# Filling the expert gate tables in DRAM with indirect adding transfers from GpSimd, in place of one-hot matmuls on TensorE

## The chip, the cores and the metric

The kernel runs on one core of a Trainium2 chip, as one program. The metric is the device time of one execution in microseconds (us). Names of engines: PE is TensorE, DVE VectorE, ACT ScalarE, POOL GpSimd; SP is the engine that issues most DMAs.

## The reference

Two layers, each an attention mixer and then a feed-forward of experts, on one sequence of 256 tokens and 2048 features. The change lies in the second part (`peer_ffn`), which for each token picks 16 of 16,384 experts for each of 8 heads:

```python
s1, i1 = lax.top_k(s[..., 0, :], PEER_TOPK)        # 16 best of 128 keys, side 1
s2, i2 = lax.top_k(s[..., 1, :], PEER_TOPK)        # side 2
cand = (s1[..., :, None] + s2[..., None, :]).reshape(b, L, PEER_HEADS, PEER_TOPK * PEER_TOPK)
cidx = (i1[..., :, None] * N_KEYS + i2[..., None, :]).reshape(...)
top_s, pos = lax.top_k(cand, PEER_TOPK)            # 16 of the 256 pairs
eidx = jnp.take_along_axis(cidx, pos, axis=-1)
g = jax.nn.softmax(top_s, -1)
...
h = jnp.einsum('td,tkd->tk', xt, u[et])
a = gt * jax.nn.gelu(h, approximate=False)
return jnp.einsum('tk,tkd->td', a, v[et])
```

The kernel does not gather rows of `u` and `v`. It computes the hidden value of every expert for every token, multiplies it by a table of gates (zero for each pair of token and expert that was not chosen, the sum of the gates where several heads chose the same one), and multiplies the product with the whole of `v`.

## The kernel before, in words

All large products are made in float32 from two rounded parts: ACT rounds a tile to its high part (`split_hi`, `hi<-raw`), DVE subtracts to get the low part (`split_lo`, `lo<-raw,hi`), and PE multiplies high and low parts. Weights come in tiles of 1 MB (`raw`, four buffers); each tile is two halves. SP loads a tile as soon as the halves that lay in its buffer have been split (`load` waits on `lo_done`), and splits run four halves ahead of PE.

Of a layer, two stages matter here. In the **u stage**, 128 tiles of `u_t` are taken, 256 halves: for each half PE runs 8 matmuls of 512 columns (L464) and 8 of 256 (L466). A body is 8 halves, so the stage has 32 bodies; `quarter` is 8 bodies. Every tile gives the hidden values of 128 experts, which go through Gelu on ACT and to `gelu_scratch` in DRAM (L954). In the **v stage**, 128 tiles of `v_t` are taken; for each half PE runs 12 matmuls of 512 columns (L691 to L693). For each tile SP first fetches the stored Gelu values and a piece of the gate table (`side`, L395 and L396), and DVE multiplies them (`product`), ACT and DVE split the product (`a_high`, `a_low`). SP issues in program order, so the loads of `v_t` stand behind the first four pairs of side loads.

The gates are made inside the u stage, in blocks `b` of 128 tokens. In quarter 1 DVE routes block 0, one head per body (`route_body`: top 16 of each side, top 16 of 256 sums, lookup of the key numbers), a loop over heads, for which POOL copies each head's scores (`copy_keys`). In quarter 2 the table of block 0 is built: the key numbers and gates are transposed on PE (L674) to `sel_t`; then for each pair of tokens, one of 64 `gate_step`s: POOL writes the one-hot rows of the first key (`first_keys`, L1094 and L1097), DVE those of the second key times the gate (`second_keys`, L1567), ACT their low part (`low_part`, L970), PE multiplies them (L656, two matmuls of 256 columns), ACT and DVE put the 128 by 128 result into `gates` in SBUF (`place_gates` L963, `add_low` L1575). Quarters 3 and 4 do the same for block 1, and in quarter 3 ACT also turns the finished block 0 over and stores it to DRAM in 16 pieces (`stage`, L977). The order on each engine is that of the program text; semaphores tie the engines together. At the end of the u stage DVE has the last three `add_low`s and then the first products ahead of PE's first matmul of the v stage.

Of the kernel before, what the change touches and what calls it, by code (L numbers as in the profile page):

```python
# [8 lines left out]
F32 = mybir.dt.float32  # L9
# [118 lines left out]
def build(nc, x_in, w_in, w_out, wq, keys, u_t, v_t, ln, sinks, lamp, subg, layer_consts,  # L128
# [10 lines left out]
    a_dram = nc.dram_tensor("gates_scratch", [NKEY, P, P], F32, kind="Internal").ap()  # L139
    g_dram = nc.dram_tensor("gelu_scratch", [NKEY, P, L], F32, kind="Internal").ap()  # L140

    with ExitStack() as ctx:
# [10 lines left out]
        SCR_OFFSET = 16512 + 4 * (NB * D + 2 * DC * L + NRAW * TILE + 2 * NSPLIT * HT + 16384)  # L153
# [6 lines left out]
        key_cols = [small[:, 64 + i * 2:66 + i * 2] for i in range(4)]  # L160
# [6 lines left out]
        key_now = sb("key_now", [P, 2, NKEY])  # L167
# [33 lines left out]
        assert at <= 16384  # L201
# [6 lines left out]
        gates = arena[:, :].rearrange("p (t i) -> p t i", i=NKEY)  # L208

# [23 lines left out]
        TG = 2  # L233
        STEPS = P // TG
        quarter = N_U // BODY // 4
        assert quarter == PH
        STEPS_OF = {0: (0,), 1: (1,), 2: (2, 3), 3: (4,), 4: (5, 6), 5: (7,), 6: (8,)}
        PER_BODY = sum(len(k) for k in STEPS_OF.values())
        BUILD = quarter - 1
        assert 1 + BUILD * PER_BODY == STEPS  # L240
        RING = 3

        def steps_at(b, i, j):
            if i == 0:
                return [b * STEPS] if j == BODY - 1 else []
            return [b * STEPS + 1 + (i - 1) * PER_BODY + k for k in STEPS_OF.get(j, ())]

        def built_at(b, i, j):
            return [n + RING for n in steps_at(b, i, j) if n + RING < (b + 1) * STEPS]

        PIECES = 16
        ROWS = NKEY // PIECES
        one_hots = nc.alloc_sbuf_tensor_at("one_hots", [P, 2048], F32R, offset=SCR_OFFSET)
        more_hots = sb("more_hots", [P, 512], F32R)
        oh1 = [t[:, i * 256:(i + 1) * 256].rearrange("p (t n) -> p t n", n=NKEY) for t in (one_hots, more_hots) for i in range(2)]
        oh2 = [one_hots[:, 512 + i * 512:512 + (i + 1) * 512].rearrange("p (t r n) -> p t r n", r=2, n=NKEY) for i in range(RING)]
        gate_rows = [scr[:, i * 1024:(i + 1) * 1024].rearrange("p (i t) -> p i t", t=P) for i in range(2)]
        gate_hi, gate_share = cand[:, 0:P], cand[:, P:2 * P]
# [39 lines left out]
        with nc.Block() as block:  # L298
            for layer in range(DEPTH):
# [37 lines left out]
                def _(sp):  # L337
# [48 lines left out]
                    with sp.Fori(0, 4 * quarter) as i:  # L386
                        for j in range(NRAW):
                            load(tiles(u_t), AT_U, i, j)
# [1422 lines left out]
```

## Time and profile before

| | |
|---|---|
| time, median of 3 runs | 3876.05 us (3875.96 to 3878.84) |
| span of the profiled execution | 3879.7 us |
| its own timed value | not among the three; only its span is known |
| PE busy | 3830.7 us, 99% |
| DVE, ACT, POOL busy | 71%, 56%, 15% |
| moved by DMA | 807.13 MB, mean 208 GB/s |

The profile is one execution recorded by the hardware. Times are from the start of the span. Busy PE time is that of the pipelined matmuls, whose recorded durations overlap: their real pace is the distance between starts. The granted clock of PE is given as a share of 2.4 GHz.

### The profile page before, as it was taken

The numbers are of one execution on the slowest core, as the hardware profiler recorded it, in microseconds if no ns is written. First come the engines' busy times: TensorE is split into PE (matmuls) and PEld (weight loads), VectorE is DVE, ScalarE is ACT, GpSimd is POOL, SyncE is SP. The second block draws the span as 40 slices with busy tenths as digits, with TensorE's granted clock in tenths as the row PEclk, the third lists the DMA queues.
The fourth block names the chain that finished last, engine by engine and source line by source line (L and its number), as shares of the span: only waits on it lengthen the run. The fifth ranks groups of instructions, "written<-read, shape, count | busy, mean of one in ns | idle before, by whom it ended". The sixth has DMA issues, their size and how long they took to land.

```text
span 3879.7 us, 62117 instructions
## 1 busy us (share of the span) xinstructions
PE 3830.7 (99%) x19796; PEld 3244.8 (84%) x19796; DVE 2745.4 (71%) x5272; ACT 2172.5 (56%) x3609; POOL 575.7 (15%) x844
## 2 busy tenths in 40 slices
PE   9999999999999999999999999999999999999997
PEld 7778888888888888888787788888888888888886
DVE  7765688778877666666687666887788766666666
ACT  5674455776676444444456644457767764444443
POOL 1000000750174000000011000017402730000000
PEclk9999999999999999999999999999999999999999
DMA  6445566557755666666654455665577556666664
GB/s 227 161 144 195 185 204 211 196 197 248 252 193 203 231 231 228 227 227 230 226 171 155 141 207 176 212 212 194 200 251 247 190 208 230 231 230 228 227 228 168
DMA packets 244209, 807.13 MB, mean 208 GB/s; under 512 B 24928, under 2 KB 157536, under 8 KB 159328
## 3 DMA queue, kind: packets, MB, share of 16 engines
q1 hardware_dynamic: 173920, 754.87, 55.6%
q10 hardware_dynamic: 70144, 50.35, 4.0%
q8 instruction: 88, 1.44, 0.1%
q14 instruction: 57, 0.47, 0.0%
HBM read 752.69 MB, written 52.43 MB: 208 GB/s over the span
## 4 chain that ended last, share of the span: by engine, by line
PE 94%; DVE 4%; ACT 1%; DMA 0%; issue 0%; POOL 0%; ACTq 0%; DVEq 0%; SPq 0%
PE bank L464 26%; PE bank L466 13%; PE bank L691 12%; PE bank L692 12%; PE bank L693 12%; PE bank L478 5%; PE bank L480 5%; PE bank L479 5%; PE bank L656 2%; DVE lo L1143 1%; PE bank L506 1%; PE bank L519 1%; PE bank L535 0%; PE bank L633 0%; PE bank L491 0%
## 5 line engine op out<-in xcount | busy, mean ns | idle before, releaser
L1143 DVE TENSOR_TENSOR lo<-raw,hi 128x1024 fp32r<-128x1024 f32 x1312 | 1616.8, 1233 | 937.2 <-ACT hi L746 913.4
L746 ACT ACTIVATE hi<-raw 128x1024 fp32r<-128x1024 f32 x1312 | 1387.2, 1060 | 1335.4 <-PE bank L693 758.6
L464 PE MATMUL bank<-xhl,hi 128*128 128x512 f32 x4608 | 1188.7, 393 | 0.5
L464 PEld LDWEIGHTS bank<-xhl,hi 128*128 128x128 f32 x4608 | 814.0, 189 | 135.0 <-DVE gelu_out L1444 1.3
L691 PE MATMUL bank<-hi,xhl 128*128 128x512 f32 x2048 | 798.3, 390 | 4.5 <-DVE xhl L1599 4.5
L692 PE MATMUL bank<-lo,xhl 128*128 128x512 f32 x2048 | 798.1, 390 | 0.0
L693 PE MATMUL bank<-hi,xhl 128*128 128x512 f32 x2048 | 798.0, 390 | 0.0
L466 PEld LDWEIGHTS bank<-xhl,lo 128*128 128x128 f32 x4608 | 654.9, 190 | 62.8
L466 PE MATMUL bank<-xhl,lo 128*128 128x256 f32 x4608 | 671.6, 282 | 0.0
L691 PEld LDWEIGHTS bank<-hi,xhl 128*128 128x128 f32 x2048 | 385.2, 188 | 85.6 <-issue 4.4
L693 PEld LDWEIGHTS bank<-hi,xhl 128*128 128x128 f32 x2048 | 385.2, 188 | 80.2
L692 PEld LDWEIGHTS bank<-lo,xhl 128*128 128x128 f32 x2048 | 385.1, 188 | 80.0
L478 PE MATMUL bank<-hi,xhl 128*128 128x512 f32 (+1 forms) x896 | 360.1, 402 | 2.3 <-DVE xhl L1161 2.3
L480 PE MATMUL bank<-hi,xhl 128*128 128x512 f32 (+1 forms) x896 | 349.9, 391 | 0.0
L479 PE MATMUL bank<-lo,xhl 128*128 128x512 f32 (+1 forms) x896 | 348.6, 389 | 0.0
L1097 POOL TENSOR_SCALAR more_hots<-iota_k,small 128x128 fp32r<-128x128 f32 x256 | 229.5, 909 | 12.1
L1097 POOL TENSOR_SCALAR one_hots<-iota_k,small 128x128 fp32r<-128x128 f32 x256 | 225.9, 895 | 12.2
L947 ACT ACTIVATE gelu_out<-bank 128x256 f32<-128x256 f32 x256 | 98.7, 385 | 193.4 <-PE bank L466 159.5
L478 PEld LDWEIGHTS bank<-hi,xhl 128*128 128x128 f32 x896 | 169.0, 189 | 37.8 <-issue 4.7
L480 PEld LDWEIGHTS bank<-hi,xhl 128*128 128x128 f32 x896 | 168.8, 188 | 35.7
L479 PEld LDWEIGHTS bank<-lo,xhl 128*128 128x128 f32 x896 | 169.4, 189 | 31.0
L970 ACT ACTIVATE one_hots<-one_hots,cand 128x128 fp32r<-128x128 f32 x512 | 171.0, 394 | 36.6 <-ACT gelu_out L952 36.6
(165 smaller groups left out, 2571.5 us busy)
## 6 DMA issues: line engine op xcount, KB each, us to landing
raw<-u_t SPq DMA_DIRECT2D x256, 1024.0 KB, 5.0
raw<-v_t SPq DMA_DIRECT2D x256, 1024.0 KB, 4.8
raw<-w_in SPq DMA_DIRECT2D x80, 1024.0 KB, 4.9
raw<-w_out SPq DMA_DIRECT2D x32, 1024.0 KB, 4.8
raw<-wq SPq DMA_DIRECT2D x32, 1024.0 KB, 4.8
gelu_scratch<-gelu_out ACTq DMA_DIRECT2D x256, 128.0 KB, 3.8
scr<-gelu_scratch SPq DMA_DIRECT2D x256, 128.0 KB, 4.5
gates_scratch<-scr ACTq DMA_DIRECT2D x32, 512.0 KB, 4.6
```

The costliest lines, as they stand in the source:

```text
L464: pe.matmul(acc[:], w, xhl[:, c, :, :].rearrange("p a t -> p (a t)"), start=(c == 0), stop=False)
L466: last = pe.matmul(acc[:, L:2 * L], w, xh[:, c, :], start=False, stop=(c == DC - 1))
L478: pe.matmul(banks[b][:, 0:width], st_h, mh, start=(c == first_c), stop=False)
L479: pe.matmul(banks[b][:, 0:width], st_h, ml, start=False, stop=False)
L480: last = pe.matmul(banks[b][:, 0:width], st_l, mh, start=False, stop=(c == last_c))
L691: pe.matmul(y, a_h, vh, start=start, stop=False)
L692: pe.matmul(y, a_h, vl, start=False, stop=False)
L693: last = pe.matmul(y, a_l, vh, start=False, stop=stop)
L746: act.activation(hi[j % NSPLIT][:], half, ACT.Copy).then_inc(hi_done, 1)
L970: last = act.activation(oh2[s % RING][:, t, 1, :], oh2[s % RING][:, t, 0, :].bitcast(F32), ACT.Identity, scale=gate_share[:, col:col + 1])
L1097: last = pool.tensor_scalar(oh1[p][:, t, :], iota_k[:], key_cols[p][:, t:t + 1], None, ALU.is_equal)
L1143: dve.tensor_tensor(lo[j % NSPLIT][:], half, hi[j % NSPLIT][:].bitcast(F32), ALU.subtract).then_inc(lo_done, 1)
```

## The change: tables filled by GpSimd's adding transfers

There is now one gate table of 128 x 128 x 256 float32 per layer, in DRAM, for both token blocks. SP fills it with zeros in quarter 1 (16 transfers of 1 MB from an SBUF region of zeros, two per body). DVE routes block 0 in quarter 1 and block 1 in quarter 2, its 16 bodies written out head by head and reading the scores where they lie. After each block DVE turns the chosen key numbers into addresses (`slots`: expert number times 256 plus token), and POOL issues for each of the 128 selections (8 heads x 16) an indirect transfer of 128 single weights, one per token, which adds them in DRAM. Since two heads may choose the same expert, the 16 transfers of a head wait for those of the head before. Transposes, one-hot rows, `gate_step`s, placing, adding and staging are gone on all engines. In the v stage `gate_in` is 128 x 256 from DRAM, and `product` is one instruction instead of two.

```diff
-    a_dram = nc.dram_tensor("gates_scratch", [NKEY, P, P], F32, kind="Internal").ap()
+    gate_dram = [nc.dram_tensor(f"gates_scratch{i}", [NKEY, P, L], F32, kind="Internal").ap() for i in range(DEPTH)]
...
+        zeros = arena[:, 15360:16384]
...
+        ZERO_TILES = 8
+        N_ZERO = NKEY // ZERO_TILES
+        N_SCATTER = 16 * PK
...
+                    def zero(n):
+
+                        tables = gate_dram[layer][bass.ds(n * ZERO_TILES, ZERO_TILES)]
+                        rows = tables.rearrange("i p t -> (i p t)").rearrange("(a r c) -> a r c", a=P, c=1024)
+                        sp.dma_start(rows, zeros.unsqueeze(1).to_broadcast([P, ZERO_TILES * L // 1024, 1024])).then_inc(zeroed, 16)
...
+                    with sp.Fori(0, quarter) as i:
                         for j in range(NRAW):
                             load(tiles(u_t), AT_U, i, j)
-                    sp.wait_ge(gates_out, 16 * PIECES)
+                            if j % 2:
+                                zero(i * 2 + j // 2)
+                    with sp.Fori(quarter, 4 * quarter) as i:
+                        for j in range(NRAW):
+                            load(tiles(u_t), AT_U, i, j)
+                    for s in scattered:
+                        sp.wait_ge(s, PH * N_SCATTER)
...
+                        sp.dma_start(gate_in[j], gate_dram[layer][bass.ds(m, 1)].rearrange("a p t -> (a p) t")
+                                     ).then_inc(side_got[j], 16)
...
-                    def gate_step(s):
...
-                            build_gates(b, 0, j)
...
+                        pool.memset(zeros, 0.0).then_inc(zeros_set, 1)
...
-                    def first_keys(s, p, first=False):
...
+                    def scatter(b, h):
+
+                        if h:
+                            pool.wait_ge(scattered[b], h * N_SCATTER)
+                        for k in range(h * PK, (h + 1) * PK):
+                            pool.indirect_dma_start(out=gate_dram[layer].rearrange("i p t -> (i p t)").unsqueeze(1),
+                                                    out_offset=bass.IndirectOffsetOnAxis(ap=slots[:, b, k:k + 1], axis=0),
+                                                    in_=sel[:, 2, b, k:k + 1], in_offset=None,
+                                                    bounds_check=NE * L - 1, compute_op=ALU.add).then_inc(scattered[b], 16)
+
+                    pool.wait_ge(zeroed, 16 * N_ZERO)
...
+                        pool.wait_ge(routed, b + 1)
+                        for h in range(PH):
+                            scatter(b, h)
...
-                            return key_now[:, s, :], top_v[:, s, :], top_i[:, s, :]
+                            return key_s[b][:, 2 * h + s, :], top_v[:, s, :], top_i[:, s, :]
...
+                            if b and h == 0:
+                                weigh_block(0, j)
...
+                        mark(dve.scalar_tensor_tensor(out=number, in0=number, scalar=float(NKEY), in1=sel[:, 0, b, :],
+                                                      op0=ALU.mult, op1=ALU.add))
...
-                    def second_keys(s):
...
-                    def add_low(s):
...
+                        mark(dve.tensor_scalar(slots[:, b, :], number, float(L), token[:, b:b + 1], ALU.mult, ALU.add))
+                        n = mark(dve.tensor_tensor(top_s, top_s, small[:, 56:64].unsqueeze(2).to_broadcast([P, PH, PK]), ALU.mult))
+                        own(n)
+                        dve.sem_inc(routed, 1)
...
-                        dve.tensor_tensor(prod[m % 2][:, 0:P], gelu_in[m][:, 0:P], gate_in[m], ALU.mult)
...
+                        dve.tensor_tensor(prod[m % 2], gelu_in[m], gate_in[m], ALU.mult).then_inc(prod_done, 1)
...
+                    for b in range(NB):
+                        for h in range(PH):
+                            route_body(b * PH + h, b, h)
+                    for j in range(BODY):
+                        step_ahead(NB * PH, j)
+                        weigh_block(1, j)
+                    with dve.Fori(NB * PH + 1, 4 * quarter - 1) as i:
                         for j in range(BODY):
...
+                            step_ahead(i, j)
+                    for j in range(BODY):
+                        if j == BODY - 1:
                             product(0, 0, first=True)
                             product(0, 1, first=True)
                             a_low(0, 0)
-                            build_split(quarter - 1, NB - 1, j, last=True)
...
+                        step_ahead(4 * quarter - 1, j, last=True)
```

Three places of the order of instructions follow. The first is PE's, in the first body of quarter 2 (L464 and L466 are one half, `one_hots` belongs to the gate steps), as it was before:

```order
L464 MATMUL bank<-xhl,hi 128x512 x7
L466 MATMUL bank<-xhl,lo 128x256 x8
L656 MATMUL bank<-one_hots 128x256 [waits oh2_low_0,oh1_done_0]
L656 MATMUL bank<-one_hots 128x256
L464 MATMUL bank<-xhl,hi 128x512 [waits summed_0,lo_done_0]
L464 MATMUL bank<-xhl,hi 128x512 x7
L466 MATMUL bank<-xhl,lo 128x256 x8
```

Now halves follow each other with nothing between them, in one loop over bodies 1 to 31. The second is DVE's, from the last half of the u stage to its first `a_low` (L1599), before:

```order
L1143 TENSOR_TENSOR lo<-raw,hi 128x1024 [waits hi_done_0]
L1575 TENSOR_TENSOR arena<-arena,bank 128x256 [waits gate_high_0] x3
L1592 TENSOR_TENSOR scr<-scr 128x128 [waits side_got0_0,gate_evac_0]
L1593 TENSOR_TENSOR scr<-scr,arena 128x128
L1592 TENSOR_TENSOR scr<-scr 128x128 [waits side_got1_0]
L1593 TENSOR_TENSOR scr<-scr,arena 128x128
L1599 TENSOR_TENSOR xhl<-scr,xhl 128x256 [waits ah_done_0]
```

and the same place in the changed kernel:

```order
L1035 TENSOR_TENSOR lo<-raw,hi 128x1024 [waits hi_done_0] x2
L1465 TENSOR_TENSOR scr<-scr 128x256 [waits side_got0_0]
L1465 TENSOR_TENSOR scr<-scr 128x256 [waits side_got1_0]
L1469 TENSOR_TENSOR xhl<-scr,xhl 128x256 [waits ah_done_0]
```

The three additions, which waited for the last gate matmuls, are gone from ahead of the products. The third is POOL's queue in the changed kernel, from the rotary additions of the attention part on (the transfers of block 0's heads 0 and 1; six more heads and block 1 follow in the same form):

```order
L989 TENSOR_TENSOR scr<-scr 128x512 [waits rope_parts] x14
L1003 DMA gates_scratch<-sel,slots 4194304x1 [waits routed_0,zeroed_0]
L1003 DMA gates_scratch<-sel,slots 4194304x1 x15
L1003 DMA gates_scratch<-sel,slots 4194304x1 [waits scattered0_0]
L1003 DMA gates_scratch<-sel,slots 4194304x1 x15
```

POOL now issues 256 transfers a layer and nothing else in the u stage, and SP's side loads, with all of `v_t` behind them, wait for the last of them.

## Rows read from the trace of the kernel before

**Rows 1.** The page: span, its busy times, and the chain that ended last.

```profile
span 3879.7 us, 62117 instructions
PE 3830.7 (99%) x19796; PEld 3244.8 (84%) x19796; DVE 2745.4 (71%) x5272; ACT 2172.5 (56%) x3609; POOL 575.7 (15%) x844
...
PE 94%; DVE 4%; ACT 1%; DMA 0%; issue 0%; POOL 0%; ACTq 0%; DVEq 0%; SPq 0%
```

**Rows 2.** Windows: 51 halves of quarter 1, quarter 1, both u stages, both v stages.

```profile
core 0: us, PE busy (x) PEld busy (x) DVE busy (x) ACT busy (x) POOL busy (x), PEclk, DMA share, GB/s
479.32:621.79 142.47, 142.47 (x817) 125.36 (x817) 122.71 (x299) 69.26 (x101) 2.83 (x7) 1.00 0.58 199
...
479.32:1233.50 754.18, 751.81 (x4359) 662.49 (x4358) 622.14 (x1384) 503.38 (x922) 258.58 (x400) 1.00 0.61 210
2408.08:3161.79 753.71, 751.66 (x4358) 662.36 (x4358) 622.44 (x1384) 502.99 (x922) 257.68 (x400) 1.00 0.61 211
...
479.32:658.10 178.78, 178.78 (x1025) 157.32 (x1025) 155.49 (x381) 87.29 (x127) 3.23 (x8) 1.00 0.58 200
```

**Rows 3.** Timeline of PE, quarter 2: start, us, line, count.

```profile
804.71 2.00 PE L464 MATMUL bank<-xhl,hi 128*128 128x512 f32 x8
...
807.50 0.40 PE L656 MATMUL bank<-one_hots,more_hots 128*128 128x256 f32 x2
807.74 2.00 PE L464 MATMUL bank<-xhl,hi 128*128 128x512 f32 x8
```

**Rows 4.** Timeline at the end of the first u stage.

```profile
1230.34 1.11 PE L466 MATMUL bank<-xhl,lo 128*128 128x256 f32 x8
1230.75 1.08 DVE L1575 TENSOR_TENSOR arena<-arena,bank 128x256 f32<-128x256 f32 x3
...
1233.50 0.47 PE L691 MATMUL bank<-hi,xhl 128*128 128x512 f32 x1 [2.05 <-DVE xhl L1599]
```

**Rows 5.** Windows of the first matmuls of each v stage (columns as in rows 2).

```profile
1233.50:1236.00 2.50, 2.50 (x8) 2.00 (x9) 1.91 (x4) 2.10 (x3) 0.00 (x0) 0.66 0.18 57
1236.00:1238.00 2.00, 2.00 (x7) 1.59 (x6) 0.43 (x1) 0.61 (x3) 0.00 (x0) 0.57 0.01 3
...
1240.00:1245.00 5.00, 5.00 (x24) 4.14 (x23) 2.82 (x6) 2.43 (x3) 0.00 (x0) 1.00 0.94 370
...
3162.00:3166.00 4.00, 4.00 (x12) 3.17 (x12) 2.15 (x4) 2.51 (x5) 0.00 (x0) 0.60 0.11 37
```

**Rows 6.** Timeline: the gates of block 0 ready; SP's queue near the u stage's end.

```profile
669.41 0.29 DVE L1548 TENSOR_TENSOR sel<-sel,small 128x128 f32<-128x128 f32 x1
...
1197.74 0.34 SPq L395 DMA_DIRECT2D scr<-gelu_scratch  x1
...
1201.19 0.43 SPq L396 DMA_DIRECT2D scr<-gates_scratch  x1
1203.33 18.67 SPq L353 DMA_DIRECT2D raw<-v_t  x4
```

**Rows 7.** POOL by line: ns min/median/max; and in 690 to 830 us.

```profile
L1097 POOL TENSOR_SCALAR one_hots<-iota_k,small x256: 602/607/1664, 674.9 to 3145.1; 128x128 fp32r<-128x128 f32 x128
...
L1097 POOL TENSOR_SCALAR more_hots<-iota_k,small 128x128 fp32r<-128x128 f32 x52 | 48.5, 945 | 2.5
```

**Rows 8.** DVE's split by line, in 690 to 830 us and in 480 to 654 us.

```profile
L1143 DVE TENSOR_TENSOR lo<-raw,hi 128x1024 fp32r<-128x1024 f32 x45 | 55.8, 1240 | 28.3 <-ACT hi L746 28.3
...
L1143 DVE TENSOR_TENSOR lo<-raw,hi 128x1024 fp32r<-128x1024 f32 x61 | 74.5, 1221 | 16.3 <-ACT hi L746 8.4 <-DVE sel L1499 5.0
```

**Rows 9.** DMA: ACT's queue (packets, MB, share of 16 engines); issues, us to landing.

```profile
q10 hardware_dynamic: 70144, 50.35, 4.0%
...
raw<-v_t SPq DMA_DIRECT2D x256, 1024.0 KB, 4.8
...
gelu_scratch<-gelu_out ACTq DMA_DIRECT2D x256, 128.0 KB, 3.8
```

**Rows 10.** The issue of that store on ACT's queue, ns min/median/max.

```profile
L954 ACTq DMA_DIRECT2D gelu_scratch<-gelu_out x256: 338/339/393, 490.6 to 3162.7; - x128
```

More of the change, by code:

```diff
@@ L1030, in _ @@
                                 act.activation(sel[:, 2, b, :], sel[:, 2, b, :], ACT.Exp).then_inc(gate_exp, 1)
[L1031 to L1039 removed]
+                    with act.Fori(NB * quarter + 1, 4 * quarter - 1) as i:
+                        for j in range(BODY):
+                            half_body(i, j)
                     def a_high(i, m):
@@ L1470, in _, with step_ahead, weigh_block @@
                     split_lo(AT_U, 0, NSPLIT - 1)
+                    def step_ahead(i, j, last=False):
+                        if j % 2:
+                            add_cross(i, j // 2)
+                        ahead = j + NSPLIT
+                        if last and ahead >= BODY:
+                            split_lo(AT_V, 0, ahead % BODY)
+                        else:
+                            split_lo(AT_U, i + ahead // BODY, ahead % BODY)
+                    def weigh_block(b, j):
+                        if j == 0:
+                            gate_weights(b)
+                        if j == 2:
+                            gate_sums(b)
                     def route_body(i, b, h):
@@ L1516, in route_body @@
                                 top8(*side(1), 8)
[L1517 to L1518 removed]
+                                then(dve.tensor_copy(key_num[:], top_i[:]))
                             elif j == 3:
@@ L1599, in a_low @@
                         dve.tensor_tensor(al[m % 2], prod[m % 2], ah[m % 2].bitcast(F32), ALU.subtract).then_inc(al_done, 1)
-                    def build_split(i, b, j, last=False):
-                        ahead = j + NSPLIT
-                        if j % 2:
-                            add_cross(i + (2 * b + 1) * quarter, j // 2)
-                        if b == NB - 1 and last and ahead >= BODY:
-                            split_lo(AT_V, 0, ahead % BODY)
-                        else:
-                            split_lo(AT_U, i + (2 * b + 1) * quarter + ahead // BODY, ahead % BODY)
@@ L1627, in last_build_body @@
-                    def last_build_body():
-                        for j in range(BODY):
-                            if j < BODY - 1:
-                                build_split(quarter - 1, NB - 1, j, last=True)
-                                build_gates(NB - 1, BUILD, j)
-                                continue
-                            build_gates(NB - 1, BUILD, j)
-                            dve.wait_ge(gate_evac, NB * STEPS)
+                    if not layer:
+                        dve.wait_ge(iota_in, 16)
+                        own(mark(dve.tensor_tensor_reduce(out=cand[:, 0:P], in0=ident[:], in1=iota_k[:], scale=1.0, scalar=0.0,
+                                                          op0=ALU.mult, op1=ALU.add, accum_out=token[:, 0:1])))
+                        own(mark(dve.tensor_scalar(token[:, 1:2], token[:, 0:1], float(P), None, ALU.add)))
```

243 lines of the change are left out of this document (24 added, 219 removed).

## Prediction

> **What bounds the kernel now.** I read the page first: PE is busy for 99% of the span and makes 94% of the chain that ended last, DVE 4% [rows 1]. So only time on PE's path counts, and everything else is judged by whether it can make PE wait. Next the windows: the two u stages, in which the change lies, last 754.18 and 753.71 us, with PE busy for all but 2.4 and 2.1 us [rows 2]. The first 142.47 us of the first one hold 817 matmuls, 51 halves of 16 [rows 2]: a half takes 142.47 / 51 = 2.7935 us when PE has nothing else, while DVE routes. The timeline in quarter 2 then shows two matmuls of a gate step between halves: the next half starts 807.74 - 804.71 = 3.03 us after the one before, 0.24 us more [rows 3]. And at the end of the stage PE stands idle for 2.05 us by its row, waiting for the first `a_low`, because three additions (L1575) are ahead of the products on DVE [rows 4]. After that gap PE is granted 0.66 and 0.57 of its clock for 4.5 us, that is the 1.2 GHz level for most of it; in the second layer 0.60 for 4 us [rows 5].
>
> **What is removed from PE.** Each u stage is 256 halves, by the bare pace 256 x 2.7935 = 715.1 us. Against the measured stages that is 39.0 us less in the first layer and 38.6 us in the second [rows 2]. Of this the 128 gate steps of a layer are 128 x 0.24 = 31 us [rows 3], the gap at the end some 2 us; the rest, some 6 us, is what double steps, transposes and ACT's staging cost, and I don't need to part it, since all of it goes. The gap should close: in the changed order the products wait only for side loads, which landed long before, and the split half ahead of them. What remains for DVE and ACT after the last half but one is a split, a Gelu, a rounding and a subtraction, which fit in the last half's 2.79 us. Without the gap I also take the slow clock away: (1 - 0.66) x 2.5 + (1 - 0.57) x 2.0 = 1.7 us in the first layer and (1 - 0.60) x 4 = 1.6 us in the second [rows 5]. Sum: 39.0 + 38.6 + 3.3 = 80.9 us.
>
> **What is added, and what hides it.** SP's zero transfers bring 16.8 MB into quarter 1, which lasts 178.78 us at 200 GB/s and a DMA share of 0.58 [rows 2]: 94 GB/s more make 294, under the 370 GB/s that a stretch reaches at a share of 0.94 [rows 5]. They stand between loads on SP's queue; a load lands in 4.8 us [rows 9], a buffer has the time of four tiles, some 22 us. Price nothing; if the cover were gone, loads would be late by the few us of each zero transfer. The v stage gets 64 KB more per tile of 1.2 MB: nothing. DVE now routes in 16 bodies running; in quarter 1 it is busy for 155.49 of 178.78 us, 87%, and PE doesn't wait [rows 2], so the second set costs nothing by itself. A block's two address instructions and POOL's one more clearing at the start are below 1 us each and off the path.
>
> **The scatters.** The one price that the trace doesn't show is c, the time that POOL's queue needs per indirect transfer of 128 weights. The budget: gates of block 0 are ready at 669.41 + 0.29 [rows 6] plus half a microsecond for addresses, 670 us. Block 1 is ready 16 bodies after 479.32, plus the same 12 us: 849 us. The stage now ends at 479.3 + 715.1 = 1194 us. The first half of `v_t` is rounded three halves before, at 1186; its load takes 4.8 us, and the eight side loads ahead of it 3.9 us of SP's queue (1197.74 to 1201.62) [rows 6, 9], so POOL must have finished by 1177. Sixteen groups end with a wait for landing, 15 of them before more work; with 3.8 us for one, the landing of the store nearest in size [rows 9], these are 57 us. So 256 c + 57 must be under 1177 - 670 = 507: **c up to 1.76 us is hidden**; block 1 alone (128 c + 27 under 328) would allow 2.35. If c is more, SP's queue is late for `v_t`, and PE waits for the whole excess. The bounds of c from rows: below, 0.34 us, what a transfer's issue takes on ACT's queue [rows 10]; above, 3.8 us, if each one kept the queue until it had landed [rows 9]. Nearest are POOL's own instructions with 128 results per partition: 0.60 us at best, 0.95 on average beside a busy DVE, 1.66 at worst [rows 7]. An indirect transfer has an address to read and two ends to write for each of 128 weights; I take one and a half times the mean, an estimate of 1.45 us. Then POOL ends at 670 + 371 + 57 = 1098, 79 us before it is needed.
>
> The spread from 0.60 to 1.66 us in that row [rows 7], with DVE's splits hardly moved at 1240 against 1221 ns [rows 8], shows who gives way when both want SBUF: POOL. The Trainium skill (SBUF — State Buffer, section SBUF: two separate sides) says that POOL and VectorE share one port pair that is held for a whole instruction, and that POOL can't write the descriptors of its own transfers while a VectorE instruction in a two-port mode holds it. The trace agrees as far as POOL waits; that scatters would wait too, no row here shows. If that rule took hold with every split, the time would be the 4277 us that rival A has for it.
>
> **Rivals.** *A, slower: POOL's queue is too slow.* Above c = 1.76 PE waits for 256 c - 450 us per layer; it eats the 40.5 us of gain per layer at c = 1.92. At c = 2.2 the time is 3876.05 - 80.9 + 2 x 113 = 4021 us. If each scatter sits out one of DVE's splits first, c is 1.45 + 1.24 = 2.7 [rows 8] and the time 4277; at 3.8 (no landing waits on top) 2 x 466 - 81 = 851 us more, 4727 (the sitting out has 0.10 of A's chance). For it: a margin of only 0.3 us over my estimate, POOL being slow at everything here, DVE at 87% in quarter 2. Against it: all nearest rows lie under 1.76. Beside it, the Trainium skill (DMA: Bandwidth & Descriptors, section Anatomy of one DMA — SWDGE (gpsimd) path) gives a transfer from POOL about 2.0 us of fixed time; if these did not overlap, 256 x 2.0 would end near 1182, 5 us late, and the time would be 3805 us; no row here shows it. Chance of A 0.30, of which 0.05 is for c from 1.76 to a little over 1.92: 0.03 still faster, 0.02 the same.
>
> *B, slower: the DMA engines choke on single weights.* A layer has 32,768 additions, 2048 for each of 16 engines, each a read and a write in DRAM. Packets of ACT's queue take 0.04 x 16 x 3879.7 us / 70144 = 35 ns [rows 1, 9]; two per addition are 2048 x 70 ns = 143 us of an engine's 507, a share of 0.28 beside 0.58. It fits. It stops fitting at (1 - 0.58) x 507 / 2048 = 104 ns per addition. At 200 ns an engine has 0.58 x 715 + 410 + 45 for zeros = 870 us of work in 715: 155 us late per layer, 4105 us. Chance 0.10.
>
> *C, less gain: scatters hold up DVE in quarter 2.* DVE has 178.78 - 155.49 = 23.3 us free there [rows 2], 0.18 us for each of 128 scatters. At 0.4 us each, 28 us per layer go onto PE's path: 3851 us. Against it: only 19 ns more per split while POOL ran its one-hot instructions [rows 7, 8]. Chance 0.06.
>
> *Hidden as forecast:* 0.54.
>
> **How the numbers follow.** The profile's span, 3879.7 us, is 3.7 us above the median of the timed runs; what lies around it isn't touched, and I subtract from the median: 3876.05 - 80.9 = 3795 us. For the likeliest case alone the range is 3785 (staging and double steps hid more of ACT than I see) to 3812 (the gap stays, some waits in quarter 1). To leave out no more than 2 in 10 I go up to c = 2.2 of rival A, 4021, which takes half of it and half of B with it: 3785 to 4020. About 0.2%, 8 us, is what a measurement of this kernel can tell from no change. Faster: 0.54 + 0.06 + 0.03 of A's mild part = 0.63; within 8 us: 0.02; slower: 0.25 + 0.10 = 0.35.
>
> **What would show it.** In the profile after: no idle stretch of PE at the start of the v stage and no granted clock under 1 there; u stages of 715 us; DVE's split no longer than 1.24 us. The last scatter issued before 1177 us, and the distance of two scatters' issues in a group gives c at once: below 1.76 the forecast stands. It is wrong if PE's first matmul of the v stage waits for a side load or `v_t`, if landings of `raw<-u_t` grow from about 5 us towards 20 during the scatters (rival B), or if PE waits for `lo` in quarter 2 (rival C).

## The result, and the profile after

| | before | after |
|---|---|---|
| time, median of 4 runs each | 3876.68 us | 3920.61 us (3917.01 to 3923.54) |
| span of the profiled execution | 3879.7 us | 3915.2 us |
| PE busy | 99% | 96% |
| POOL busy | 15% | 23% |

The ratio is 1.0111, with a 95% interval from 1.0099 to 1.0123: the change made the kernel 1.1% slower. The forecast was 3795 us, in a range of 3785 to 4020 us.

The page of the kernel after (busy times; then busy tenths and granted clock in 40 slices; then queues; then the chain that ended last, beside [rows 1]):

```profile
span 3915.2 us, 58717 instructions
PE 3757.8 (96%) x19272; PEld 3179.5 (81%) x19272; DVE 2483.1 (63%) x4239; ACT 1869.4 (48%) x2805; POOL 918.4 (23%) x557
PE   9999999999993999999999999999999949999998
PEclk9999999999996999999999999999999979999999
q0 software_dynamic: 73728, 0.29, 4.3%
PE 65%; POOL 16%; issue 10%; DMA 4%; DVE 3%; ACT 1%; POOLq 0%; SPq 0%; ACTq 0%; DVEq 0%
...
L1003 POOL DMA_INDIRECT gates_scratch<-sel,slots x512 | 858.1, 1676 | 1140.6 <-issue 611.9 <-DVEq L1459 437.7 <-DMA gates_scratch<-sel,slots 91.0
```

PE lost its one-hot work, and two slices of its row fell to 3 and 4 tenths: the two places where a u stage ends and a v stage begins. There the granted clock dips too. In the chain PE fell from 94% to 65%; POOL and "issue", time in which an engine waited for nothing that the profile shows, have 26% now, where they had 0%. The last row, from the groups by line (busy us, mean ns, idle before and what ended it), is the indirect transfers; the 91.0 us at its end are the 28 waits for a landing. The windows of the first layer put numbers on it (columns as in [rows 2]: length, busy time of PE, PEld, DVE, ACT, POOL with their counts, granted clock, DMA share, GB/s):

```profile
478.79:1192.79 714.00, 714.00 (x4089) 628.53 (x4089) 506.57 (x984) 347.16 (x511) 396.67 (x236) 1.00 0.76 224
1194.00:1255.00 61.00, 0.01 (x1) 0.04 (x1) 5.04 (x7) 4.36 (x7) 30.27 (x20) 0.54 0.39 90
1255.00:1260.00 5.00, 5.00 (x12) 3.94 (x13) 2.05 (x4) 3.43 (x6) 0.00 (x0) 0.50 0.10 36
```

The u stage is all PE, at full clock, and lasts what was forecast. Then PE has nothing for 61 us, and after that it runs 5 us at a granted clock of 0.50, the 1.2 GHz level. Read backwards through the timelines of PE, SP's queue and POOL, the end of that gap is a chain (start, duration, what; idle time before it and its releaser in brackets):

```profile
1192.77 1.11 PE L455 MATMUL bank<-xhl,lo 128*128 128x256 f32 x8
1254.99 0.77 PE L653 MATMUL bank<-hi,xhl 128*128 128x512 f32 x1 [61.11 <-DVE xhl L1469]
```
```profile
1236.69 0.34 SPq L383 DMA_DIRECT2D scr<-gelu_scratch  x1
...
1240.40 2.13 SPq L327 DMA_DIRECT2D raw<-v_t  x4
```
```profile
1231.87 1.55 POOL L1003 DMA_INDIRECT gates_scratch<-sel,slots  x1 [0.30 <-issue]
1233.72 1.55 POOL L1003 DMA_INDIRECT gates_scratch<-sel,slots  x1 [0.30 <-issue]
```

PE waits for the first `a_low` on DVE, that for the side loads and `v_t`, those stand on SP's queue behind its wait for `scattered`, and the last transfer starts on POOL at 1233.72. The 512 transfers run at this pace:

```profile
704.16 2.20 POOL L1003 DMA_INDIRECT gates_scratch<-sel,slots  x1 [0.30 <-issue]
711.14 1.55 POOL L1003 DMA_INDIRECT gates_scratch<-sel,slots  x1 [4.77 <-DMA gates_scratch<-sel,slots]
712.99 1.58 POOL L1003 DMA_INDIRECT gates_scratch<-sel,slots  x1 [0.30 <-issue]
714.88 1.55 POOL L1003 DMA_INDIRECT gates_scratch<-sel,slots  x1 [0.30 <-issue]
...
811.85 1.56 POOL L1003 DMA_INDIRECT gates_scratch<-sel,slots  x1 [2.32 <-issue]
```

A transfer holds POOL for 1.55 us at best and 1.676 us on average, with 0.30 us between two: c = 1.98 us, where 1.76 was the limit. The row with 4.77 us is a landing wait, at a change of head. The row at 811.85 is something else: a pause inside a head, for which the profile names no cause. The first layer adds up row by row: from 670.89 to 1233.72 + 1.55 are 564.4 us. POOL is busy for 428.3 of them, 235 gaps of 0.30 us are 71.2, the 14 landing waits are 50.5 (3.6 us each, from 2.3 to 5.0), and six pauses inside heads, behind transfers 60, 113, 120, 188, 241 and 248 of the layer, are 14.3. In the second layer the 14 landing waits are 40.5 us, six pauses at the same transfers 16.2, and PE's gap is 53.67 us.

### The profile page after: what moved, and what is told of

It is laid out like the page before. It is cut to its first block, busy times and chain, and to the rows that moved or that the text cites. A ratio compares the mean times of both kernels' runs of the same rounds, so it can differ in the third digit from the quotient of the medians.

```text
span 3915.2 us, 58717 instructions
## 1 busy us (share of the span) xinstructions
PE 3757.8 (96%) x19272; PEld 3179.5 (81%) x19272; DVE 2483.1 (63%) x4239; ACT 1869.4 (48%) x2805; POOL 918.4 (23%) x557
## 3 DMA queue, kind: packets, MB, share of 16 engines
q0 software_dynamic: 73728, 0.29, 4.3%
## 4 chain that ended last, share of the span: by engine, by line
PE 65%; POOL 16%; issue 10%; DMA 4%; DVE 3%; ACT 1%; POOLq 0%; SPq 0%; ACTq 0%; DVEq 0%
POOL gates_scratch L1003 16%; PE bank L653 12%; PE bank L654 12%; PE bank L655 12%; PE bank L453 9%; PE bank L467 5%; PE bank L469 5%; PE bank L468 5%; PE bank L455 4%; DMA gates_scratch<-sel,slots 3%; DVE lo L1035 1%; PE bank L495 1%; PE bank L508 1%; PE bank L524 0%; PE bank L622 0%
## 5 line engine op out<-in xcount | busy, mean ns | idle before, releaser
L1035 DVE TENSOR_TENSOR lo<-raw,hi 128x1024 fp32r<-128x1024 f32 x1312 | 1613.7, 1230 | 1153.3 <-ACT hi L708 1144.4
L1003 POOL DMA_INDIRECT gates_scratch<-sel,slots x512 | 858.1, 1676 | 1140.6 <-issue 611.9
L653 PE MATMUL bank<-hi,xhl 128*128 128x512 f32 x2048 | 799.7, 390 | 115.1 <-DVE xhl L1469 115.1
L653 PEld LDWEIGHTS bank<-hi,xhl 128*128 128x128 f32 x2048 | 385.6, 188 | 196.3 <-issue 115.1
L1336 DVE TENSOR_TENSOR gelu_out<-bank,gelu_out 128x256 f32<-128x256 f32 x256 | 108.8, 425 | 126.9 <-ACT gelu_out L909 122.8
```

The lines of the kernel that those rows point to most:

```text
L653: pe.matmul(y, a_h, vh, start=start, stop=False)
L1003: pool.indirect_dma_start(out=gate_dram[layer].rearrange("i p t -> (i p t)").unsqueeze(1), out_offset=bass.IndirectOffsetOnAxis(ap=slots[: ...
L1035: dve.tensor_tensor(lo[j % NSPLIT][:], half, hi[j % NSPLIT][:].bitcast(F32), ALU.subtract).then_inc(lo_done, 1)
L1336: dve.tensor_tensor(gelu_out[m % 2][:], bank[m % 2][:, 0:L], gelu_out[m % 2][:], ALU.add).then_inc(summed, 1)
```

## The experiments

Their question: is the lateness the length of POOL's queue, and what is c made of? Each run is given with its time, the median of the kernel before on the same chip, and what its trace shows of L1003.

**Half of the transfers.**

```diff
-        N_SCATTER = 16 * PK
+        N_SCATTER = 16 * PK // 2
...
-                        for k in range(h * PK, (h + 1) * PK):
+                        for k in range(h * PK, h * PK + PK // 2):
```

> Each head's transfers cut from 16 to 8 (half of the gate weights are left out of the tables). Theory, the POOL queue is too slow (256 transfers at 1.98 us and 15 landing waits take 564 us where 507 are free): now 128 transfers, about 8 x 1.98 + 3.8 = 19.6 us per head, 157 us per block; block 0 is done at about 828 us, block 1 at about 995 us in layer 0, long before the u stage ends at 1192.8, so both PE gaps of 61 us go: about 3920 - 2 x 61 - 3 = 3795 us. Rival, the v stage's start is late for something else (the gelu stores, the side loads, the last raw loads): the gap stays and the time is 3900 or more. Rival, the weights choke the DMA engines: the time falls by half of the loss only.

Measured 3801.09 us (before: 3879.52). PE's gap was 1.01 us, still behind `a_low`:

```profile
1195.16 0.47 PE L653 MATMUL bank<-hi,xhl 128*128 128x512 f32 x1 [1.01 <-DVE xhl L1469]
```

The stall is the transfers' own; nothing else was late. The time is 6 us above the expectation, but not by the 256 transfers that are left: the next run, without any, has the same time.

**No transfers.** L1003's loop and SP's wait for `scattered` are taken out.

> No transfers at all, the rest as in the changed kernel, zeroing in quarter 1 too (leaves out the gates: the tables stay zero). This gives the sum without its scatter term. Both stage ends should be as in the run with 8 transfers per head: 3795 to 3802 us. If it is well under 3800 us, even hidden transfers cost something (DVE or DMA contention); if not, they are free where they are hidden.

Measured 3801.06 us (before: 3878.11), the same as with 256 transfers. Transfers that are hidden cost nothing, and this is the floor of the change: its span is 3799.3 us, 80.4 us under that of the profiled execution of before. By the timed runs on its own chip the saving is 77.1 us (3878.11 to 3801.06). The window of its first u stage:

```profile
478.80:1194.00 715.20, 714.98 (x4096) 629.25 (x4094) 510.39 (x990) 351.56 (x518) 0.00 (x0) 1.00 0.66 231
```

PE is busy for 714.98 us with 4096 matmul records, and POOL for none.

**64 weights per transfer, then 32.**

```diff
-                                                    out_offset=bass.IndirectOffsetOnAxis(ap=slots[:, b, k:k + 1], axis=0),
-                                                    in_=sel[:, 2, b, k:k + 1], in_offset=None,
+                                                    out_offset=bass.IndirectOffsetOnAxis(ap=slots[0:64, b, k:k + 1], axis=0),
+                                                    in_=sel[0:64, 2, b, k:k + 1], in_offset=None,
```

> Each transfer carries 64 weights instead of 128 (tokens 64 to 127 of each block are left out), the count stays 512. If the price of a transfer on POOL is a fixed one, it stays at 1.55 + 0.30 us, and the time at about 3920 us. If it goes by the weights it carries, 1.55 becomes 0.78, a layer's 256 transfers take 256 x 1.1 + 57 = 340 us and hide: about 3795 us. A price that is half fixed gives 1.16 + 0.30, 256 x 1.58 + 57 = 461 us under the 507 free: also about 3795 us, told apart by the duration in the trace.

> Each transfer carries 32 weights (tokens 32 to 127 of each block are left out), the count stays 512. A transfer of 128 weights takes 1.547 us on POOL, one of 64 takes 1.397: by a straight line 1.25 us fixed and 2.3 ns per weight, so 1.32 us here. If POOL's price goes in steps (by packets of 64), it stays at 1.40. Time: a queue shorter by another 256 x 0.08 = 20 us per layer than with 64 weights, so 3859 - 2 x 20 = about 3820 us, or 3859 if it goes in steps.

Measured 3859.15 us with 64 and 3849.84 us with 32 (before: 3879.52 and 3880.15). One row of each by tile (min, median, max in ns):

```profile
L1003 POOL DMA_INDIRECT gates_scratch<-sel,slots x512: 1392/1397/2433, 672.0 to 3120.4; - x171
```
```profile
L1003 POOL DMA_INDIRECT gates_scratch<-sel,slots x512: 1297/1298/2352, 670.2 to 3111.4; - x171
```

The price is nearly fixed: 1.547, 1.397 and 1.298 us for 128, 64 and 32 weights, 2 to 3 ns a weight on some 1.2 us. All three prices stated for 64 weights (1.55, 1.16 and 0.78 us) missed, the fixed one by the least. The time with 32 weights was 30 us over my straight line, for two reasons. The mean fell only from 1.549 to 1.513 us, less than the median: between 887 and 898 us, for one, every third transfer took 2.08 us. And the 28 landing waits grew from 108.5 us with 64 weights to 120.9. Per layer that is 9 us less and 6 us more, where I had 20 us less.

```profile
887.00 1.30 POOL L1003 DMA_INDIRECT gates_scratch<-sel,slots  x1 [0.31 <-issue]
888.61 1.30 POOL L1003 DMA_INDIRECT gates_scratch<-sel,slots  x1 [0.30 <-issue]
890.21 2.08 POOL L1003 DMA_INDIRECT gates_scratch<-sel,slots  x1 [0.31 <-issue]
```

The 2.08 us led to the run with short splits below.

**Writing instead of adding.**

```diff
-                                                    bounds_check=NE * L - 1, compute_op=ALU.add).then_inc(scattered[b], 16)
+                                                    bounds_check=NE * L - 1).then_inc(scattered[b], 16)
```

> The same 512 transfers write instead of adding (where two picks of a token name one expert, the last one stays instead of their sum). If the adding is what makes a transfer take 1.55 us on POOL, or its landing 3.5 us, both fall and the stall of 61 us shrinks; my theory is that POOL's time is the writing of 128 descriptors and does not know the adding: 1.55 us and 0.30 us stay, the landing shortens by at most 1 us (15 x 1 us per layer), the time is 3890 to 3920 us.

Measured 3801.95 us (before: 3879.52). My expectation fell: the adding is priced on POOL's queue. By tile, and grouped by line (busy us, mean ns):

```profile
L1003 POOL DMA_INDIRECT gates_scratch<-sel,slots x512: 968/975/2014, 671.5 to 3002.6; - x171
```
```profile
L1003 POOL DMA_INDIRECT gates_scratch<-sel,slots x512 | 582.6, 1138 | 1179.7 <-issue 605.4 <-DVEq L1459 438.6 <-DMA gates_scratch<-sel,slots 135.7
```

The writing form takes 0.975 us where the adding form takes 1.547: the adding costs 0.57 us. With its mean of 1.138 and the gap of 0.30, c would be 1.44 us, and the first layer's last transfer starts at 1112.74 us, hidden. The landing waits are longer here, 135.7 us for 28 where the adding form has 91.0. The two forms also differ in what they hand to the DMA engines:

```profile
q0 software_dynamic: 16384, 0.29, 0.3%
```

These are 16384 packets where the adding form has 73728. Divided by 512 transfers, the adding form has 144 packets each, one per weight and 16 more, and the writing form 32.

**Writing 64 weights.**

> 64 weights per transfer, written and not added (tokens 64 to 127 are left out, duplicates aren't summed). With 128 weights the adding makes 1.547 us of 0.975. If that is a fixed price of the adding form, this takes 1.397 - 0.57 = 0.83 us; if it is one per weight (4.5 ns), the adding costs 0.29 at 64 and this would take 1.11 us, more than the 0.975 of 128 weights, so the fixed part must then sit in the writing form too: 0.9 to 1.0. Time 3801 us in any case, the queue is hidden.

Measured 3801.83 us (before: 3880.15); the median is 0.910 us. So the adding costs 0.49 us at 64 weights and 0.57 at 128: mostly a fixed price of the form. It does not follow the packets: with 64 weights q0 has 40960 of them when adding and 16384 when writing, 48 more per transfer, and with 128 weights it is 112 more. What POOL does in that time no run shows.

**Blocks in turns.**

```diff
-                    for b in range(NB):
-                        pool.wait_ge(routed, b + 1)
-                        for h in range(PH):
-                            scatter(b, h)
+                    pool.wait_ge(routed, 1)
+                    for h in range(PH // 2 + 1):
+                        scatter(0, h)
+                    pool.wait_ge(routed, NB)
+                    for h in range(PH // 2 + 1, PH):
+                        scatter(1, h - PH // 2 - 1)
+                        scatter(0, h)
+                    for h in range(PH // 2 - 1, PH):
+                        scatter(1, h)
```

> Same result as the reference. Order of the 16 groups on POOL's queue alone is changed: from head 5 of block 0 on the two blocks take turns, so that six of the fourteen landing waits per layer lie beside the other block's transfers. Count, price and start of the transfers stay. Theory (lateness is the plain sum of queue time and landings): 6 x 3.25 = 19.5 us per layer less idle, the PE gap falls from 61 to about 42 us: 3920 - 39 = 3881 us. Rival: the landings only overlap with something that POOL would wait for anyway, the gap stays at 61: 3920 us.

Measured 3860.20 us (before: 3878.11), ratio 0.9954, interval 0.9937 to 0.9971. The direction is right, but the gain is 20 us more than expected. The landing waits did what they were priced at: 28 waits with 91.0 us became 16 with 51.3, which is 39.7 us less where 2 x 19.5 were expected. Two things fell that I had held fixed: the transfers' busy time, from 858.1 to 847.9 us, and the pauses inside heads, from 30.5 to 18.6 us over both layers. Why they fell stays open. The gap of the first layer fell by 31.5 us, from 61.11 to this:

```profile
1222.98 0.76 PE L653 MATMUL bank<-hi,xhl 128*128 128x512 f32 x1 [29.64 <-DVE xhl L1474]
```

**Two tables by turns.**

```diff
-                        if h:
-                            pool.wait_ge(scattered[b], h * N_SCATTER)
+                        landed = scattered[2 * b + h % 2]
+                        table = gate_dram[(layer + h) % 2]
+                        if h > 1:
+                            pool.wait_ge(landed, h // 2 * N_SCATTER)
...
-                            pool.indirect_dma_start(out=gate_dram[layer].rearrange("i p t -> (i p t)").unsqueeze(1),
+                            pool.indirect_dma_start(out=table.rearrange("i p t -> (i p t)").unsqueeze(1),
```

> Even and odd heads add into two different tables, so a head waits for the landing of the head before the last alone (the odd heads' gates land in the other layer's table and are left out of the product). All 14 landing waits go: 45 us per layer less, 256 transfers take 671 + 506 = 1177 to 1190 us where the u stage ends at 1192.8: the gap falls from 61 to 10 to 16 us: 3820 to 3835 us. If the landing wait were not idle queue time the time would stay near 3920 us.

Measured 3801.51 us (before: 3878.11). That is under the 3820 to 3835 us expected. No wait for a landing is left in the trace; the last transfer of the first layer starts at 1167.09 us, just in time, and its queue is 497.9 us long instead of 564.4. Of the 66.5 us the landing waits are 46.3 (50.5 less 14 gaps of 0.30). The rest is again busy time (428.3 to 419.0 us) and pauses (14.3 to 2.0). By an estimate from these numbers the landing waits alone would have left a gap of some 15 us a layer, and with 3801 + 2 x 15 us the kernel would still have been faster than before.

**Short splits.**

```diff
-                        dve.tensor_tensor(lo[j % NSPLIT][:], half, hi[j % NSPLIT][:].bitcast(F32), ALU.subtract).then_inc(lo_done, 1)
+                        for at in (0, HT // 2):
+                            cols = slice(at, at + HT // 2)
+                            last = dve.tensor_tensor(lo[j % NSPLIT][:, cols], half[:, cols], hi[j % NSPLIT][:, cols].bitcast(F32), ALU.subtract)
+                        last.then_inc(lo_done, 1)
```

> Same result as the reference. The changed kernel with each of DVE's splits of 128x1024 written as two of 128x512. Theory from the trace: a transfer that POOL begins while a split runs stands until 0.14 us before the split's recorded end, one begun before it or beside other DVE work takes 1.55 us whatever DVE does. Then the longest falls from 2.59 to about 2.05 us, the mean from 1.68 to about 1.62, a layer's queue gets some 15 us shorter and the time falls by 20 to 40 us to 3880 to 3900 us, as long as DVE's two extra starts don't make PE wait in the routing quarters. Rival, the stretch is contention in DRAM or on the DMA ring: the longest stay at 2.6 us, and the time at 3920 us.

The observation behind it, in the trace of the kernel after (POOL, then DVE):

```profile
841.48 1.97 POOL L1003 DMA_INDIRECT gates_scratch<-sel,slots  x1 [0.30 <-issue]
843.75 2.22 POOL L1003 DMA_INDIRECT gates_scratch<-sel,slots  x1 [0.30 <-issue]
```
```profile
843.33 1.23 DVE L1035 TENSOR_TENSOR lo<-raw,hi 128x1024 fp32r<-128x1024 f32 x1 [0.52 <-ACT hi L708]
```

The transfer at 843.75 begins 0.42 us into a split that ends at 844.56, and takes 0.67 us more than 1.55: 0.14 us less than the 0.81 that were left of the split. Between 880 and 1190 us of that trace, each of the 96 transfers begun while DVE was idle took 1.55 to 1.57 us, also where a split began just behind; of the 49 begun inside a split, the 11 with over 0.5 us of it left took 2.13 to 2.58 (a twelfth, begun 0.03 us into it, 1.55).

Measured 3907.03 us (before: 3880.15). By tile:

```profile
L1003 POOL DMA_INDIRECT gates_scratch<-sel,slots x512: 1542/1548/2048, 671.1 to 3169.0; - x171
```

The longest is 2.05 us, as expected, and the mean 1.597: the mechanism holds. The time fell by less than expected, to 3907 us and not to 3880 to 3900. The transfers' busy time shrank by 20 us per layer (858.1 to 817.5 us over both), but the 28 landing waits grew from 91.0 to 114.6 us and the pauses inside heads from 30.5 to 38.9, which takes 16 us per layer back; why they grew stays open.

**Only the zeroing earlier.** The 16 zero transfers of a layer go behind every second load of `w_out` and `wq` (two loops of 4 x 4 loads) instead of those of quarter 1.

> Same result as the reference. Only the zeroing moves (w_out and wq stages instead of quarter 1 of the u stage). Nothing that sets the end moves: 3920 us. It separates the two halves of the early version: if this is slower, the zeroing costs PE something in the w_out or wq stage; if faster, the zeroing in quarter 1 did cost.

Measured 3916.14 us (before: 3878.11), no difference from 3920.61 that one run could show: PE's gap 59.0 against 61.1 us. The zeroing's place is free.

**Only the gates earlier: groups of four heads.** The weighing (maximum, exponential, sum, slots) is done after heads 4 and 8 of each block, for 64 of its columns, instead of once for all 128:

```diff
-                            if b and h == 0:
-                                weigh_block(0, j)
+                            n = b * PH + h
+                            if n and n % GROUP == 0:
+                                weigh_group(n // GROUP - 1, j)
...
-                    for b in range(NB):
-                        pool.wait_ge(routed, b + 1)
-                        for h in range(PH):
-                            scatter(b, h)
+                    for n in range(NB * PH):
+                        if n % GROUP == 0:
+                            pool.wait_ge(routed, n // GROUP + 1)
+                        scatter(n // PH, n % PH)
```

> Same result as the reference. The gates per four heads as in the early version, but the zeroing stays in quarter 1 of the u stage, where its last transfer is issued at 616.6 us and lands 8.7 us later: 625 us. Theory (a layer's queue is one block of some 575 to 582 us that moves with its start; PE is late by what it starts its last transfer after 1173.6 us): last transfer at 1200 to 1206 us, PE waits for 27 to 33 us per layer: 3801 + 2 x (30 + 1.6 of slow clock) = 3864 us. If the early start of the groups alone were enough: 3801 us; if the zeroing held the transfers up further (both write to DRAM): up to 3916 us.

Measured 3864.74 us (before: 3877.28), the expected time, out of two errors that cancel. The first transfer waits for the zeroing, as expected, but until 639 us (the last zero transfer is issued at 629.12, not at 616.6); the queue behind it is 570 us long instead of 575 to 582. First and last transfer of the layer:

```profile
639.13 1.67 POOL L1003 DMA_INDIRECT gates_scratch<-sel,slots  x1 [406.24 <-DMA gates_scratch<-arena]
```
```profile
1207.13 1.55 POOL L1003 DMA_INDIRECT gates_scratch<-sel,slots  x1 [0.31 <-issue]
```

So each of the two halves of the early start is short of the deadline by itself.

**Both: the early version.**

> Same result as the reference. Softmax and slots are worked out per four heads (four groups per layer), so that the first transfers can leave after four heads of routing, and the zeroing moves ahead, into the w_out and wq stages. Theory (the queue's work is as long as before, but starts earlier): first transfer at about 478.8 + 5 x 22.35 - 16 = 575 us instead of 671, the last about 564 us later, at 1139 us, before the u stage's end at 1192.8: both PE gaps go, about 3795 us. Rival: the zeroing in the w_out and wq stages (16.8 MB beside loads that take 0.56 to 0.58 of the DMA engines) delays their loads, each us of PE idle there counts; or the added DVE and ACT operations in the routing bodies (DVE is busy 155 of 179 us) make PE wait: 3800 to 3840 us.

Measured 3801.07 us (3799.94 to 3802.43, 4 runs; before: 3879.52), ratio 0.9798, interval 0.9781 to 0.9816: faster than before by 2.0%, than the changed kernel by about 3%, and the same as with no transfers at all. Its page's rows of the engines and of L1001 (the same transfer, two lines up), and the first and last transfer of the first layer:

```profile
PE 3754.9 (99%) x19272; PEld 3176.9 (84%) x19272; DVE 2485.1 (65%) x4267; ACT 1881.3 (50%) x2817; POOL 941.9 (25%) x557
L1001 POOL DMA_INDIRECT gates_scratch<-sel,slots x512 | 881.5, 1722 | 974.4 <-issue 539.6
```
```profile
581.62 1.67 POOL L1001 DMA_INDIRECT gates_scratch<-sel,slots  x1 [348.23 <-issue]
...
1162.05 1.55 POOL L1001 DMA_INDIRECT gates_scratch<-sel,slots  x1 [0.31 <-issue]
```

The time is 6 us above the expectation and at the floor. The queue is 582 us long here, 18 more than in the kernel after, since more transfers run beside routing (mean 1.722 us); it only starts 89 us sooner.

One relation holds through all the runs that are late: last transfer's start against PE's gap, first layer.

| run | last start | PE's gap | start less gap |
|---|---|---|---|
| changed kernel | 1233.72 | 61.11 | 1172.6 |
| zeroing early | 1232.72 | 59.02 | 1173.7 |
| short splits | 1226.70 | 51.95 | 1174.8 |
| gates early | 1207.13 | 33.35 | 1173.8 |
| 64 weights | 1202.06 | 27.97 | 1174.1 |
| in turns | 1202.04 | 29.64 | 1172.4 |
| 32 weights | 1197.59 | 23.85 | 1173.7 |

Every us after about 1173.6 is a us of PE's; the two-table run (1167.09) and the early version (1162.05) are before it and have no gap beyond 1.01 us.

## Why the prediction was wrong

**What bounds the kernel, and what is removed: right.** The u stage has PE at work for 714.98 us of a window of 715.20 us in the run without transfers, where 256 halves were to give 715.1. Against the profiled execution of before that run's span is 80.4 us shorter; the sum was 80.9. The last microsecond of the gap [rows 4] did not close: 1.01 of 2.05 us stay, in every hidden run. The slow clock behind it [rows 5] did go: granted 1.00 from 1195 us on in the run without transfers. I took this saving from the median of the timed runs, though, not from the profiled span that it was worked out of; 3879.7 - 80.9 + 1.8 (a timed value stands 1.8 us above its span here) would have been 3801, the measured floor, instead of 3795. That profiled execution was one of the longer ones of the kernel before: between medians on one chip the saving is 77.1 us.

**What is added, and what hides it: right.** In quarter 1, with the zeroing, PE was busy throughout (817 matmuls in 142.51 us, 290 GB/s; forecast 294); from 670 to 838 us, beside routing and transfers, too. Moving the zeroing changed nothing.

**The scatters: the step that failed.** It said: "I take one and a half times the mean, an estimate of 1.45 us. Then POOL ends at 670 + 371 + 57 = 1098, 79 us before it is needed." c was 1.98 us, and POOL ended at 1235.3. The frame of the step held: POOL's deadline, which I had put at 1177, is some 1175 (1173.6 and a last transfer of 1.55 us). That 256 x 1.98 + 57 = 564 us meets the 564.4 measured so closely is partly luck. The busy time and the plain gaps of the first layer are 499.5 us and not 507, its landing waits 50.5 and not 57 (14 of 3.6 us where I had 15 of 3.8), and the pauses of 14.3 us, which I did not know of, fill the difference. The term that was mis-sized is c, and its edge was known: the prediction had worked out 1.76. Its parts as the runs show them: 0.975 us for a writing transfer, 0.57 for the adding form, 0.13 on average for sitting out splits, 0.30 between two. Without the adding c is 1.44 us, so the estimate happens to be that of a plain indirect write. I had reasoned about the addition as two packets on a DMA engine, and put no price of it on the queue that issues it. That was the error. The 0.22 us above the limit of 1.76, 256 times a layer, turned -2% into +1.1%. The 3920.61 us lie inside the range of 3785 to 4020 us, but among the slower outcomes, to which the prediction had given 0.35; the case it forecast is not what happened.

**Rival A: this is what happened**, just past its mild form. By its formula, 256 x 1.98 - 450 = 57 us per layer; measured 61.1 in the first layer and 53.7 in the second. The four waits of this kind add up to 115.1 us over both layers (2.4 in the run without transfers), and 115.1 - 2.4 = 112.7 on 3799.3 make 3912.0. The 3.2 us left to 3915.2 are of the size of the slow clock's price after the two long gaps: behind the first, 12 matmuls start 0.43 us apart instead of 0.23, which is 2.4 us, and behind the second 7 do, 1.4 us. I had called c between 1.76 and a little over 1.92 "mild", gave it 0.05 and the whole of A 0.30; c came out at 1.98, where A makes the kernel slower. Where 0.5 us of error in a guessed price reverses the sign, 0.54 for "hidden" was too much.

Of the sitting out I had two cases, never and always (2.7 us). It was neither: only a transfer that begins inside a split waits, for what is left of it, so 0.13 us on average and not 1.24. The Trainium skill (SBUF — State Buffer, section SBUF: two separate sides) says that POOL can't write the descriptors of its own transfers while a VectorE instruction in a two-port mode holds the shared ports. The trace agrees for the start of a transfer: 2.22 us at 843.75, and the longest fell from 2.59 to 2.05 us with halved splits. Which mode the split runs in, no run here shows. In the other direction nothing was held up: from 672 to 1189 us the 149 splits that began while a transfer ran on POOL took 1.21 to 1.23 us each, and they did not lengthen the transfer.

The 2.0 us per transfer that the Trainium skill gives (DMA: Bandwidth & Descriptors, section Anatomy of one DMA — SWDGE (gpsimd) path) happened to lie near the 1.98 us here; the sum of 3805 us that the prediction made with it left out the landing waits and is not what happened. That c falls to 1.44 us without the adding shows that the agreement is one of numbers and not of causes.

**Rival B: refuted.** The page's q0 row gives 0.043 x 16 x 3915.2 / 73728 = 36.5 ns per packet, where 35 were assumed, and the count is 144 packets per transfer of 128 weights, not two per weight. Loads of `raw<-u_t` landed in 5.0 us, and with a quarter of the weights the first layer's queue was still 528.6 us long. **Rival C: refuted.** DVE's splits took 1230 ns (1233 before), and from 670 to 838 us, in quarter 2, PE was busy for 168.00 of 168.00 us.

## What to carry to other kernels

When work moves to an engine that "has time", the number to bound is that engine's queue time per instruction, times the count, against the stretch between the first input and the consumer; compute the price at which the sign turns, and if the guess lies near it (here 1.45 against 1.76, and the guess was 0.53 off), either change the design or forecast the loss as likely. Such a queue is one block: it can be made shorter or start sooner, and here starting sooner cost nothing (gates per four heads, tables zeroed two stages ahead), while fixed prices (the form of the transfer, a landing wait at every group) made up nearly all of its length, so a quarter of the weights per transfer took only 36 of 564 us off it. A cheaper transfer did not give back its whole price either, since the landing waits grew. And each saving worked out of a profiled execution belongs subtracted from that execution's own time.

## What the runs showed of the hardware

- An indirect transfer of one 4-byte weight per partition holds POOL for 1.547 us when it adds and 0.975 us when it writes (128 partitions); 1.397 and 0.910 us with 64, and 1.298 us with 32 when it adds. 0.30 us lie between two.
- The adding form makes 144 packets of 128 weights, 80 of 64 and 48 of 32 (one per weight and 16 more); the writing form makes 32 of 128 or 64 weights. A packet took 36.5 ns when adding and, by the rounded 0.3%, some 11 ns when writing.
- One that begins inside a 128x1024 subtraction on DVE is longer by what is left of the subtraction, less 0.14 us (up to 2.59 us in all); one begun before it, or in its first 0.04 us, stays at 1.55 us, and the subtraction itself isn't lengthened.
- The wait from a head's last transfer to the next head's first one, mean of 28, was longer in each run whose transfers were shorter: 3.25 us in the changed kernel (transfers of 1.676 us on average), 3.9 with 64 weights (1.549), 4.1 with short splits (1.597), 4.3 with 32 weights (1.513) and 4.8 when writing (1.138). Why stays open.
- Behind the same six of a layer's 256 transfers the changed kernel's POOL paused for 1.8 to 3.9 us inside a head; what it waited for the profile does not show.
- After 61 us of idling PE was granted 0.50 of its clock for 5 us; after 1.01 us of idling, 1.00; in the kernel before, after 2.05 us, 0.66 and 0.57 [rows 5].
